# Five edits around the first attention and the mixer of a two-block forward pass: where one root is taken, how spare products are dealt out, when a weight half is signalled, and where a norm is applied

## The reference, cut to what matters

```python
# first block, attention layer
k = rmsnorm(h @ w_k, k_norm)          # per head, 16 heads of 64
q = rmsnorm(rmsnorm(h, b_norm) @ w_q, b_q_norm)
p = softmax(q k^T / 8 + rel_bias)     # causal within 256 tokens
h = h + (p @ v) @ w_o
h = h + square(relu(rmsnorm(h, mlp_norm) @ w_up)) @ w_down
# second block, mixer
g = rmsnorm(x, norm_mix_pre)
q_mb, k_mb, v_mb, q_sw, k_sw, v_sw, q_me, gate1, gate2, gate3 = split(g @ w_in)
merged = sigmoid(gate1) * (o_mb @ w1) + sigmoid(gate2) * (o_sw @ w2) + sigmoid(gate3) * (o_me @ w3)
x = x + rmsnorm(merged @ w_out, norm_mix_post)
```

## Time and profile before

| | |
|---|---|
| median of 3 runs | 1058.41 us (1053.68 to 1058.56) |
| the profiled execution | 1058.11 us |
| its span (first to last instruction) | 1056.3 us |
| PE busy | 1020.2 us, 97% |
| DVE busy | 663.1 us, 63% |
| ACT busy | 557.0 us, 53% |
| granted TensorE clock, mean | 0.993 |
| first attention, 358 to 426 us | PE busy 55.8 of 68.0, clock 0.92 |
| norm of the mixer, 606 to 626 us | PE busy 16.5 of 20.0, clock 1.00 |

### The profile page before, as it was taken

How to read it: one execution, slowest core, us unless ns; L and a number is a source line. 1 busy time by engine, 2 the same in 40 slices (tenths; PEclk the granted TensorE clock), 3 DMA queues, 4 the chain that set the end, 5 groups by cost and what they waited for, 6 DMA issues and landing times. The chain is left out here.

```text
span 1056.3 us, 16543 instructions
## 1 busy us (share of the span) xinstructions
PE 1020.2 (97%) x6742; PEld 921.8 (87%) x6742; DVE 663.1 (63%) x950; ACT 557.0 (53%) x820; POOL 87.1 (8%) x104
## 2 busy tenths in 40 slices
PE   8999999999999978999999989999999989999997
PEld 7998999999987756899999879988899879999996
DVE  5979565555457767565555554366564648877775
ACT  6896454444455465554444453366544347555552
POOL 2610010000001210120000000000002510000000
PEclk9999999999999989999999999999999999999999
DMA  9736585556527324465555546542334626655531
GB/s 322 236 125 220 173 290 197 181 180 199 190 89 244 115 81 165 155 223 181 193 191 181 185 132 192 168 141 87 120 120 152 208 79 200 199 198 177 184 120 40
DMA packets 120275, 180.41 MB, mean 171 GB/s; under 512 B 3113, under 2 KB 93577, under 8 KB 120217
## 3 DMA queue, kind: packets, MB, share of 16 engines
q1 hardware_dynamic: 118352, 174.11, 49.9%
q0 software_dynamic: 1536, 5.36, 1.5%
q10 hardware_dynamic: 329, 0.12, 0.0%
HBM read 178.48 MB, written 1.10 MB: 170 GB/s over the span
## 5 line engine op out<-in xcount | busy, mean ns | idle before, releaser
L1064 PE MATMUL PS<-XA,whi 128*128 128x256 f32 x2512 | 458.3, 284 | 1.5 <-DVE XA L1696 1.2
L1645 DVE TENSOR_TENSOR wlo<-raw,whi 128x2048 fp32r<-128x2048 f32 x154 | 354.6, 2306 | 162.5 <-ACT whi L621 162.0
L1064 PEld LDWEIGHTS PS<-XA,whi 128*128 128x128 f32 x2512 | 394.1, 192 | 11.4 <-issue 6.2
L621 ACT ACTIVATE whi<-raw 128x2048 fp32r<-128x2048 f32 x153 | 292.0, 1910 | 129.1 <-PE PS L1109 103.7
L1064 PE MATMUL PS<-XA,wlo 128*128 128x256 f32 x1256 | 355.3, 283 | 0.0
L1064 PEld LDWEIGHTS PS<-XA,wlo 128*128 128x128 f32 x1256 | 240.7, 192 | 0.0
L1109 PE MATMUL PS<-whi,XB 128*128 128x512 f32 x736 | 209.0, 391 | 0.0
L1109 PEld LDWEIGHTS PS<-whi,XB 128*128 128x128 f32 x736 | 135.6, 188 | 26.6 <-issue 0.5
L1109 PE MATMUL PS<-wlo,XB 128*128 128x512 f32 x368 | 117.6, 390 | 0.0
L1109 PEld LDWEIGHTS PS<-wlo,XB 128*128 128x128 f32 x368 | 69.1, 188 | 14.6
L810 ACT ACTIVATE arena<-PS 128x256 f32<-128x256 f32 x64 | 24.2, 383 | 96.2 <-PE PS L1064 95.7
(11 more groups left out here) (239 smaller groups left out, 1129.7 us busy)
## 6 DMA issues: line engine op xcount, KB each, us to landing
raw<-in_w_up SPq DMA_DIRECT2D x32, 1024.0 KB, 5.4
raw<-in_w_down SPq DMA_DIRECT2D x32, 1024.0 KB, 5.0
raw<-in_w_ffn_up SPq DMA_DIRECT2D x22, 1024.0 KB, 5.1
raw<-in_w_in SPq DMA_DIRECT2D x21, 1024.0 KB, 5.3
raw<-in_w_ffn_down SPq DMA_DIRECT2D x11, 1024.0 KB, 5.0
raw<-in_w_kv SPq DMA_DIRECT2D x8, 1024.0 KB, 4.9
raw<-in_a_w_in SPq DMA_DIRECT2D x7, 1024.0 KB, 8.1
raw<-in_w_mem_kv SPq DMA_DIRECT2D x4, 1024.0 KB, 5.1
```

The costliest lines, as they stand in the source:

```text
L621: act.activation(whi[:, s, :], raw[:, s, :], ACT.Copy).then_inc(s_hi, 1)
L1064: ins = pe.matmul(PS[:, bank_of(g), 0:T], w[:, k, P * m:P * m + P], X[:, k0 + k, part, :], start=(i == 0 and part == 0 and w is hi), stop= ...
L1645: dve.tensor_tensor(wlo[:, s, :], raw[:, s, :], whi[:, s, :].bitcast(F32), ALU.subtract).then_inc(s_lo, 1)
```

## The change

There are five edits.

1. `kq_sum(KQ_K1)` moves on DVE from pair 1 to pair 0, behind `kq_scale(KQ_Q1)`; `kq_scale(KQ_K1)` from pair 2, ahead of the normalising, to the end of pair 1, between two weight halves; on ACT `kq_square(KQ_K1)` goes behind the first weight half.
2. `FILLS` and `SPLIT_AT` are dealt out anew: `fill(0)` runs between the scores of pairs 0 and 1, pair 3 has one piece, pairs 4 to 6 have three, and unit `U_O + 3` is split in pair 4 and not in pair 3. `values_out(U_V1, 1)` moves from pair 2 to pair 3.
3. The first half of a unit's high part raises a semaphore of its own, `s_whh`, and DVE's first half waits for that.
4. The mixer's norm is deferred: `add_lift` and `first_up` take the place of `add_out`, `norm` and `norm_T`; the roots are broadcast into bank 7 and copied to `rstd_row`.
5. All groups of the mixer's projection are multiplied by `rstd_row` by DVE on the way out of PSUM (15 for queries and keys, 24 for gates), the two token-major products by `dsc`. ACT takes the Tanh of a gate in SBUF afterwards, in place.

```diff
-DEFERRED = (2, 3, 4)
+DEFERRED = (2, 3, 4, 5)
...
-    if g in (G_MLP0, G_MLP0 + 1, G_MLP1, G_MLP1 + 1):
+    if g in (G_MLP0, G_MLP0 + 1, G_MLP1, G_MLP1 + 1, G_QMB, G_QMB + 1):
         return 4 + 2 * (g % 2)
...
-        FILLS = [[2, 2], [1, 1], [1, 1], [1, 1], [1, 1], [2, 1], [1, 1], [1, 1]]
-        SPLIT_AT = {0: U_K1 + 1, 1: U_V1, 2: U_V1 + 1, 3: U_O, 5: U_O + 1, 6: U_O + 2}
+        FILLS = [[1, 1], [1, 1], [1, 1], [0, 1], [2, 1], [2, 1], [2, 1], [1, 1]]
+        SPLIT_AT = {0: U_K1 + 1, 1: U_V1, 2: U_V1 + 1, 4: U_O, 5: U_O + 1, 6: U_O + 2}
+        HALVED = [u + LEAD for u in (U_K1 + 1, U_V1, U_V1 + 1, U_O, U_O + 1, U_O + 2)]
...
-            roots(SQ_NORM[5])
+            roots_deferred(SQ_NORM[5], DS_MIX, mhalf)
...
                     if part == 1:
                         ins.then_inc(s_hi, 1)
+                    elif u in HALVED:
+                        ins.then_inc(s_whh, 1)
...
                 probs_out(A)
-                if p == 0:
-                    kq_square(KQ_K1)
                 if p == 2:
                     kq_evac(KQ_K1)
                 if p in SPLIT_AT:
                     split(SPLIT_AT[p] + LEAD, part=0)
+                if p == 0:
+                    kq_square(KQ_K1)
+                if p == 3:
+                    values_out(U_V1, 1)
                 probs_out(B)
...
-            norm(5, res, [(XA, R_MIX)], added(A_MLP1))
-            two = lambda v, i: [v[:, 2 * i + m, :] for m in range(2)]
-            for i in range(2):
-                unit_a(U_QKV + i, G_QMB + 2 * i, two(qT_mb, i), scale=0.125)
...
+            lift_hi(5, [(XA, R_MIX)], U_MLP1 + MLP_UNITS - 1)
+            squares_res(SQ_NORM[5])
+            unit_b(U_QKV)
+            unit_b(U_QKV + 1)
+            act.wait_ge(s_bc, 1)
+            act.activation(rstd_row[:], PS[:, 7, 0:T], ACT.Copy).then_inc(s_row, 1)
+            for i in range(2, 11):
+                unit_b(U_QKV + i)
...
-                evac(G_G2[b] + k, BEFORE(U_G2[b]) + k + 1, g_br[b][:, k, :], ACT.Tanh, 0.5)
                 if H <= last:
                     probs_out(H)
+                act.wait_ge(s_evac, G_G2[b] + k + 1)
+                act.activation(g_br[b][:, k, :], g_br[b][:, k, :], ACT.Tanh, scale=0.5).then_inc(s_tanh, 1)
...
             score_pair(0)
-            j = 0
+            fill(0)
+            j = 1
...
-            norm_T(5)
-            for i in range(2):
-                unit_a(U_QKV + i, G_QMB + 2 * i, xready=NORM_HI[5] if i == 0 else None)
+            first_up(U_QKV, G_QMB, 5, lambda: res_T(1, A_MLP1, 4))
+            have(U_QKV + 1)
+            group(G_QMB + 2, (U_QKV + 1) % SLOTS, 0, W8, KT, XA)
+            pe.wait_ge(s_rstd, ROOTS[SQ_NORM[5]] + TT)
+            for t in range(TT):
+                ins = pe.matmul(PS[:, 7, P * t:P * t + P], dsc[:, DS_MIX + t:DS_MIX + t + 1].to_broadcast([P, P]),
+                                ident[:], start=(t == 0), stop=(t == 1), skip_group_check=True)
+            ins.then_inc(s_bc, 1)
+            group(G_QMB + 3, (U_QKV + 1) % SLOTS, 1, W8, KT, XA)
...
-                dve.wait_ge(s_hi, it * units + u + 1)
+                if part == 0:
+                    dve.wait_ge(s_whh, HALVED.index(u) + 1)
+                else:
+                    dve.wait_ge(s_hi, it * units + u + 1)
...
-                if p == 2:
-                    kq_scale(KQ_K1)
...
                     kq_scale(KQ_Q1)
-                if p == 1:
                     kq_sum(KQ_K1)
...
                 if p - 1 in SPLIT_AT:
                     split(SPLIT_AT[p - 1] + LEAD, part=1)
+                if p == 1:
+                    kq_scale(KQ_K1)
                 if p in SPLIT_AT:
                     split(SPLIT_AT[p] + LEAD, part=0)
-                if p == 2:
+                if p == 3:
                     values_out(U_V1, 1)
...
+            def rows_out(u, g, dsts, scale=1.0):
+
+                for m, dst in enumerate(dsts):
+                    dve.wait_ge(s_step, BEFORE(u) + m + 1)
+                    dve.scalar_tensor_tensor(dst, PS[:, bank_of(g + m), 0:T], scale, rstd_row[:], ALU.mult, ALU.mult)\
+                       .then_inc(s_evac, 1)
+                if u > U_QKV:
+                    split(u + LEAD)
...
                 if k % 2 == 0:
                     split(U_G2[b] + k // 2 + LEAD)
+                dve.wait_ge(s_step, BEFORE(U_G2[b]) + k + 1)
+                dve.tensor_tensor(g_br[b][:, k, :], PS[:, bank_of(G_G2[b] + k), 0:T], rstd_row[:], ALU.mult)\
+                   .then_inc(s_evac, 1)
                 if H - 1 <= last and k:
                     attn_lo(H - 1)
```

More of the change, by code:

```diff
@@ L1228, in down @@
                     tokens(s, W2, 2, XB, 2 * (j % 2), 4, 2, first, last, pieces_=True,
[L1229 removed]
+                           lift=(A_MLP0 if layer == 0 else A_MLP1))
                 def up_(i, it=0):
@@ L1982, in _ @@
             mlp(1)
-            dve.wait_ge(s_rstd, ROOTS[SQ_NORM[4]] + TT)
-            add_out(A_MLP1, U_MLP1 + MLP_UNITS - 1, DS_MLP1)
-            norm(5, res, [(XA, R_MIX)], late=U_MLP1 + MLP_UNITS - 1 + LEAD)
-            for i in range(6):
-                split(U_QKV + i + LEAD)
-            dve.wait_ge(s_step, AFTER[U_QKV + 5])
-            dve.tensor_copy(v_mb, PS[:, 6:8, :]).then_inc(s_bev, 1)
-            for i in range(6, 9):
-                split(U_QKV + i + LEAD)
-            dve.wait_ge(s_step, AFTER[U_QKV + 8])
@@ L1995, in _ @@
-            dve.tensor_copy(v_sw, PS[:, 5, 0:T].rearrange("p (t n) -> p t n", t=TT)).then_inc(s_bev, 1)
-            for i in range(9, 11):
-                split(U_QKV + i + LEAD)
+            add_lift(A_MLP1, U_MLP1 + MLP_UNITS - 1, 5, [(XA, R_MIX)], U_MLP1 + MLP_UNITS - 1 + LEAD, DS_MLP1)
+            def rows_out(u, g, dsts, scale=1.0):
[5 more added lines that the diff above has]
+                    split(u + LEAD)
@@ new lines, in _ @@
+            two = lambda v, i: [v[:, 2 * i + m, :] for m in range(2)]
+            split(U_QKV + LEAD)
+            dve.wait_ge(s_row, 1)
+            for i in range(2):
+                rows_out(U_QKV + i, G_QMB + 2 * i, two(qT_mb, i), 0.125)
+            for i in range(2):
+                rows_out(U_QKV + 2 + i, G_KMB + 2 * i, two(kT_mb, i))
+            for i in range(2):
+                split(U_QKV + 4 + i + LEAD)
+            dve.wait_ge(s_step, AFTER[U_QKV + 5])
+            for t in range(TT):
+                ins = dve.tensor_scalar(v_mb[:, t, :], PS[:, 6 + t, :], dsc[:, DS_MIX + t:DS_MIX + t + 1], None, ALU.mult)
@@ new lines, in _ @@
+            ins.then_inc(s_bev, 1)
+            for i in range(2):
+                rows_out(U_QKV + 6 + i, G_QSW + 2 * i, two(qT_sw, i), 0.125)
+            rows_out(U_QKV + 8, G_KSW, [kT_sw])
+            dve.wait_ge(s_step, AFTER[U_QKV + 8])
+            for t in range(TT):
+                ins = dve.tensor_scalar(v_sw[:, t, :], PS[:, 5, P * t:P * t + P], dsc[:, DS_MIX + t:DS_MIX + t + 1], None,
+                                        ALU.mult)
+            ins.then_inc(s_bev, 1)
+            for i in range(2):
+                rows_out(U_QKV + 9 + i, G_QME + 2 * i, two(qT_me, i), float(P) ** -0.5)
```

30 lines of the change are left out of this document (10 added, 20 removed).

## The result

The changed kernel takes 1046.75 us (median of 5 runs, 1046.34 to 1047.67) where the kernel before, on the same chip in the same rounds, takes 1056.27 (median of 5, 1053.68 to 1058.56). The ratio is 0.991, with a 95% interval from 0.9889 to 0.993: 9.5 us less, 7.4 to 11.7 by the interval. I had predicted 1049.3, range 1044.5 to 1055.0.

The account below looks back on a forecast made before the run. PE bounds the kernel, busy 1020.2 of 1056.3 us, so only its waits and low clocks can be gained. Attention -5.9 and mixer -2.9 (-4.3 + 1.2 + 0.2) give -8.8 from 1058.1: 1049.3 us, range 1044.5 to 1055.0.

Parts of the forecast that it names:

- Attention, predicted -5.9: First attention, edits 1 to 3: 7.3 us gained less 1.4 for a low clock, between -3 and -8.5.
- 8.9 us earlier, and I keep 13.6: First attention: DVE's last row maxima start at 403.6, not 412.51; the tail to the output product stays 13.6 us.
- Eight times 0.2 us of drain: First attention: drain left out at eight hand-overs, 1.6 us deducted from the 8.9, leaving 7.3.
- The second route: First attention from PE's side: waits of 9.1 us replace 12.2; with 4.2 of low clock regained, 7.3 us gained.
- The low clock at 1.4 us: First attention, pairs 0 and 1: PE's clock may fall behind two short waits, costing 1.4 us (bounds 0 and 2.8).
- Mixer norm, predicted -4.3: Mixer's norm, edit 4: 12.4 us become 7.7 by deferring, plus 0.36 for the broadcast.
- cost nothing, clock 1.00: Mixer's old norm: PE's waits of 1.5, 0.8 and 1.2 us around the transposes caused no low clock.
- First head, predicted +1.2: Head 16: DVE's last remainder stands behind the group's copy, so row maxima begin at 687.9, not 686.68; 1.2 us lost.
- Heads, predicted 0 with a slack of 1.5 us: Mixer's heads, pair at 697.61: DVE's normalising ends at 702.3, PE asks at 703.80, so nothing is lost.
- Rivals 1 and 2: First attention: clock falls more than once, 1053.5 us, chance 0.13; removed wait returns one hand-over later, 1053.0 to 1054, 0.10.
- Rival 3: Mixer's heads: DVE's queue delays every second head beyond the slack; slower, up to 1065 us; chance 0.06.
- Rival 4: Whole kernel: both gains come in full and the clock stays up, 1047 us; counted inside the forecast's 0.71 chance.

Follow-up runs that it names:

- warm_attn: The changed kernel with 11 extra, unneeded matmuls on PE in two waits of the first attention; 1047.09 us, ratio 0.9908 to the kernel before.
- heads_plus: The changed kernel with six extra DVE reductions ahead of the gate group's product in every second mixer head; 1069.16 us, ratio 1.0099 to the kernel before.
- attn_only: The kernel before with the three attention edits (1 to 3), mixer as before; 1051.13 us, ratio 0.9942.
- table_only: The kernel before with edit 2 alone (pieces and splits dealt out anew); 1056.85 us, ratio 0.9994.
- mixer_only: The kernel before with the two mixer edits (4 and 5), attention as before; 1051.87 us, ratio 0.9947.
- remainder_early: The changed kernel with DVE's remainder of the projection's last unit moved ahead of that unit's second group; 1046.12 us, ratio 0.9901 to the kernel before.
- root_only: The kernel before with edit 1 alone (second keys' sum, square and scaling moved); 1055.61 us, ratio 0.9994.
- before: The kernel before the change, unaltered, which the others are compared to; 1056.27 us beside the changed kernel.
- halves_off: The changed kernel with edit 3 undone, so DVE's first weight half again waits for ACT's second half; 1051.14 us, ratio 0.9947 to the kernel before.
- root_again: The kernel before with edit 1 alone, profiled in a second execution; 1055.85 us.
- mixer_again: The kernel before with edits 4 and 5 alone, profiled in a second execution; 1051.62 us.

## Why the prediction was right, point by point

**The sum.** 9.1 us predicted from the median shown, or 8.8 from the profiled execution; 9.5 measured in paired runs, and 11.4 between the two traces. Direction and places were right. That the total came out near is in part luck: between the traces the attention's term was 3.0 us too small, and the profiled execution before was a long one.

**Attention, predicted -5.9.** In the traces it is 67.51 to 58.64, -8.9. My schedule of DVE's turns put the last row maxima at 403.6, and they stand at 403.38. So the step "8.9 us earlier, and I keep 13.6" was the right one (the tail is 13.7), and the two deductions were wrong. "Eight times 0.2 us of drain" took off 1.6 us that don't exist. The second route, PE's waits of 9.1 us, agreed with 7.3 only because it was too pessimistic as well: they are 6.4 (and its terms as listed add up to 9.0). The low clock at 1.4 us did come, once, where I had put it; `warm_attn` shows that it costs nothing, since DVE is the later one in those turns. 5.9 + 1.6 + 1.4 = 8.9. The Trainium skill, page "TensorE: Matmul & The Clock Gate", section "A second HAM failure mode: psum-queue depth-cycling", would have the short waits cost throughput. The trace agrees in part: the clock did fall behind two of them (0.50 from 370 to 372 us). But it cost no time here, and did cost time in the feed-forward's norm and in `heads_plus`, where nothing else was late.

Measured over many runs the attention is worth -5.9 us (`attn_only` by its median), and that the number is the predicted one is luck. What I took as the kernel before was an execution with an attention of 67.5 us; others of the same code took 63.9. After the change it took 58.6 to 58.7 us in each of seven profiled executions of kernels that share it, one of which had no low clock. A part of the gain is thus that a spread of some 3.7 us is gone. By medians there is a second doubt: in `attn_only` the old mixer norm lost 1.6 us to a low clock in the one profiled execution, and how often it does is not known.

**Edit 3** I had put at 1.2 us, at the first turn. In the traces it is worth 1.9 us, nearly all at turns 3 and 5; at the first turn 0.25.

**Mixer norm, predicted -4.3.** From the output product to head 16's scores it is 259.52 before and 254.98 after: -4.5. `first_up` took 6.65 us (6.64 predicted), the transposes and the broadcast stood without a wait, and POOL's last root was there at 613.86, 9.0 us after `first_up` began (9.1 predicted). One cost of the old norm I had wrong: that its waits "cost nothing, clock 1.00". In `attn_only` and `table_only`, which still have it, the clock fell there behind the same three waits (1.5, 0.8 and 1.2 us), and from its first transposes to head 16's scores they took 72.6 and 71.6 us in place of 71.0. In the nine profiled executions with the deferred norm it never fell. That may be why `mixer_only` gains 5.2 us by its median and 3.5 by its landmarks; with so few profiles it isn't shown.

**First head, predicted +1.2; third branch, +0.2.** +0.9 and +0.1. The cause of the first is shown by `remainder_early`.

**Heads, predicted 0 with a slack of 1.5 us.** 0 was right, the slack was not: 2.2 at the pair that I read, none at head 17. At the pair itself I had the step wrong as well: I left the remainder's start where it was, and it moved 0.7 us ahead. Rival 3 was nearer than its chance of 0.06 says, since another 2.08 us in every second head cost 20 us. I had taken one pair for all eight, and priced a late pair by its wait alone; what came behind the waits, mostly low clock, cost nearly as much again (9.6 us beside 12.3).

**Rivals 1 and 2** did not come: one low clock in the first pairs, no wait at L1275, and ACT's copies cost 4.3 us and not more than 9. Rival 4 (1047) is in its number what happened, but not with the clock up, and its sum takes 0.5 us for the first head and the third branch where mine has 1.4.

## What to carry to other kernels

Where two engines hand work back and forth, lay out the later engine's turns one behind the other from durations in the trace, trust the start of the last turn, and take nothing off for hand-overs that the other engine's lateness covers. When every edit of a set moves one of two engines that wait for each other, each alone may be worth next to nothing (here -1.4 and -0.2 us by the medians, neither told from zero) and the set a lot (-5.9). Before pricing a stretch with waits of 1 us and more, look at the spread of the runs: one trace holds one draw of low clocks, and here it made a stretch 67.5 us long that took 63.9 in another execution.

## What the hardware showed that I had not expected

- Nearly the same waits, in the same order, are followed by a granted clock of 0.50 for some microseconds in one execution and by 1.00 in the next: in the attention of `root_only` no low clock in one execution and a mean of 0.92 in the other, at the mixer's old norm in two of five. In the feed-forward's norm it fell every time, but cost 1.3 to 2.8 us over the 9.13 us at full clock. The Trainium skill, page "TensorE: Matmul & The Clock Gate", section "What's actually happening", says that the number of slow matmuls at a kernel's start varies from run to run of one kernel; these traces agree as far as they show it (the 36 transposes with which every kernel here begins took 5.7 us in one execution and 7.2 in another, though the granted clock reads 1.00 there in all), and they show the same in the middle of a kernel.
- Extra matmuls in two waits of 2.7 and 1.2 us kept the clock at 1.00 and brought 2.5 us in the traces (1.8 by medians of different rounds), though PE did 15 more matmuls.
- POOL's power over 128x16 for the second keys took 4.92, 3.79, 3.69, 3.00 or 2.92 us. In seven profiles with edits 1 to 3 it was 3.00 each time, in four with the keys' sum at its old place 3.79 twice and 4.92 twice. It is long wherever it starts inside a remainder of DVE, and by nearly what is left of it: 2.00 us more with 2.14 left (`before`), 0.77 more with 0.91 left (`root_only`, `halves_off`). A remainder that starts after the power does not lengthen it (`root_again`, 2.92), nor is it held up itself for more than 0.06 us. Why `mixer_again` waited for one half and `mixer_only` for two is open.
